# Two-layer decoder trunk on one core: the input handed over in both layouts, and a first stage without transposes

## The reference

```python
def gdn_mixer(x, w_in, conv_w, a_log, dt_bias, norm_g, w_out):
    h = x @ w_in
    qkv, z, b_raw, a_raw = split(h)               # q, k, v, z: 8 heads x 128 columns each; b, a: 8 columns each
    qkv = silu(causal_depthwise_conv(qkv, conv_w))    # 4 taps per channel
    ...
    beta = sigmoid(b_raw)
    g = -exp(a_log) * softplus(a_raw + dt_bias)
    o = gated_delta_rule(q, k, v, beta, g)        # chunked recurrence per head
    return (rms_norm(o, norm_g) * silu(z)) @ w_out
x = layer_norm(ALPHA * x + y)                     # the residual uses x again, with positions along the rows
```

## Time and profile before

| | us |
|---|---|
| median of 3 runs | 1806.77 (1806.12 to 1807.46) |
| the profiled execution's own time | 1807.62 |
| its span, first to last instruction | 1805.9 |
| TensorE busy | 1708.3 (95% of the span) |
| DVE, ACT, POOL busy | 867.9, 790.4, 300.7 |
| mean granted TensorE clock | 0.978 of full speed |

### The profile page before, as it was taken

The page is one execution under the profiler, slowest core; times in us unless marked ns, Lnnn a source line. Parts: engine busy times, 40 slices in busy tenths (PEclk is TensorE's granted clock), DMA queues, the critical chain, the costliest instruction groups (busy, mean ns, idle before and its releaser), DMA issues. The chain is left out here.

```text
span 1805.9 us, 29014 instructions
## 1 busy us (share of the span) xinstructions
PE 1708.3 (95%) x11245; PEld 1303.6 (72%) x11245; DVE 867.9 (48%) x1664; ACT 790.4 (44%) x1296; POOL 300.7 (17%) x243
## 2 busy tenths in 40 slices
PE   6999999999999897979989998999999999898898
PEld 4777777787777775858877887666666665687787
DVE  3667576674766635653330300344444454565433
ACT  3557465574655732142231311465655665430411
POOL 2222132221322251200000000222221221012000
PEclk9999999999999998989989999999999999899899
DMA  5121110211101121141130201111111101050311
GB/s 131 48 53 36 31 48 12 49 37 34 48 13 38 57 95 59 35 125 44 53 107 1 71 25 36 43 33 45 44 33 42 43 22 41 19 164 28 117 44 50
DMA packets 113080, 92.87 MB, mean 51 GB/s; under 512 B 19696, under 2 KB 95664, under 8 KB 112944
## 3 DMA queue, kind: packets, MB, share of 16 engines
q1 hardware_dynamic: 112944, 91.02, 17.8%
HBM read 82.51 MB, written 8.49 MB: 50 GB/s over the span
## 5 line engine op out<-in xcount | busy, mean ns | idle before, releaser
L481 PE MATMUL gdn_unit<-part_hi,gdn_w_hi 128*128 128x512 f32 x512 | 231.8, 453 | 0.2 <-DVE gdn_w_lo L837 0.2
L483 PE MATMUL gdn_unit<-part_hi,gdn_w_lo 128*128 128x512 f32 x512 | 201.5, 394 | 0.0
L482 PE MATMUL gdn_unit<-part_lo,gdn_w_hi 128*128 128x512 f32 x512 | 200.5, 392 | 0.0
L2090 DVE CUSTOM_DVE_ANT_0 fa_probs<-fa_scores,fa_decay 128x896 f32<-128x896 f32 (+7 forms) x128 | 97.0, 758 | 121.2 <-PE fa_scores L1902 73.6
L877 DVE SCALAR_TENSOR_TENSOR x<-gdn_raw,gdn_taps,x 128x512 f32<-128x512 f32 x144 | 132.4, 919 | 21.9 <-ACT x L696 17.2
L1854 PE MATMUL fa_unit<-part_hi,fa_w_hi 128*128 128x512 f32 x256 | 115.0, 449 | 4.8 <-ACT fa_qk L2001 3.4
L446 POOL TENSOR_TENSOR gdn_w_lo<-ring,gdn_w_hi 128x1024 fp32r<-128x1024 f32 x31 | 74.6, 2408 | 265.2 <-ACT gdn_w_hi L676 265.2
L2036 ACT ACTIVATE fa_probs_t<-fa_turned 128x512 f32<-128x512 f32 (+1 forms) x96 | 52.3, 545 | 139.3 <-PE fa_turned L1919 138.7
L483 PEld LDWEIGHTS gdn_unit<-part_hi,gdn_w_lo 128*128 128x128 f32 x512 | 96.1, 188 | 21.5
L2030 ACT ACTIVATE fa_probs<-fa_probs,fa_top 128x896 f32<-128x896 f32 (+7 forms) x128 | 99.4, 777 | 22.6 <-DVE fa_top L2090 18.9
L481 PEld LDWEIGHTS gdn_unit<-part_hi,gdn_w_hi 128*128 128x128 f32 x512 | 96.8, 189 | 16.8 <-issue 3.6
(11 more groups left out here) (307 smaller groups left out, 3622.1 us busy)
## 6 DMA issues: line engine op xcount, KB each, us to landing
ring<-in_gdn_w_in_dram SPq DMA_DIRECT2D x32, 512.0 KB, 4.2
ring<-in_ple_w_gate_dram SPq DMA_DIRECT2D x32, 256.0 KB, 3.0
ring<-in_fox_w_in_dram SPq DMA_DIRECT2D x32, 256.0 KB, 3.3
ring<-in_fox_w_in_dram SPq DMA_DIRECT2D x16, 512.0 KB, 4.7
fa_decay<-c_rows_scratch SPq DMA_DIRECT2D x64, 128.0 KB, 3.0
in_x_tile<-in_x_dram SPq DMA_DIRECT2D x8, 512.0 KB, 6.8
gdn_g_bc<-g_rows_scratch SPq DMA_DIRECT2D x8, 512.0 KB, 8.6
x_scratch<-x SPq DMA_DIRECT2D x8, 512.0 KB, 2.9
```

Source lines behind the costliest of these rows:

```text
L481: pe.matmul(out, w_hi[:, j % 2, k, :], xh[:, k, ts], start=(k == 0), stop=False)
L482: pe.matmul(out, w_hi[:, j % 2, k, :], xl[:, k, ts], start=False, stop=False)
L483: mm = pe.matmul(out, w_lo[:, j % 2, k, :], xh[:, k, ts], start=False, stop=(k == KT - 1))
```

## The change

The kernel gets x twice: as before, and as `x_t`, with channels along the rows. `transpose_input` is gone, and with it its barrier and the loads `to_gdn`. In `delta_net`:

- SP issues, in this order: `load(0)`, x_t's tile 0, the b/a columns, tiles 1 to 7 of x_t, `load(1)`, the two short vectors, the taps, the gain. The raw tiles lie in buffers that are unused at that time (`x_raw`).
- ScalarE makes `high_part(0)`, then the high part of each tile, with `ab_hi` behind tile 0; VectorE makes the low parts in the same order. The wait for the short vectors moves to where they are used.
- GpSimd makes the constants here, and signals `masks_made`.
- TensorE warms up with 18 matmuls in place of 9, and then `first_products` makes, tile by tile, what steps 0 to 15 of iteration 0 made (both halves of q of head 0) and the b/a products: 12 matmuls for each tile.
- Gates are turned at step 18, summed at 36, rows turned at 40; ScalarE copies the product at step 16.

```diff
-def transpose_input(nc, x, c, xh, xl, after):
...
-AT_GATES = 2
-AT_GATES_TURNED = 6
-AT_G_SUMS = 24
-AT_G_ROWS = 28
+AT_GATES = 16
+AT_GATES_TURNED = 18
+AT_G_SUMS = 36
+AT_G_ROWS = 40
...
+        def x_raw(k):
+            return qkvz_space[:, 4 + k] if k < 4 else o_t[:, k + 1] if k < 7 else qkvz_space[:, 3]
...
+            load(0)
+            for k in range(KT):
+                sp.dma_start(x_raw(k), turned_input[0, k * P:(k + 1) * P, :]).then_inc(x_loaded[k], 16)
+                if k == 0:
+                    sp.dma_start(ab_raw, w_in[:, 4 * H * DK:4 * H * DK + 2 * H].rearrange("(k p) n -> p k n", p=P)
+                                 ).then_inc(ab_loaded, 16)
+            load(1)
...
+            constants_program(pool, step, c, ident_made, masks_made)
...
+            def first_products():
+                pe.wait_ge(w_low, 1)
+                for k in range(KT):
+                    pe.wait_ge(x_low, k + 1)
+                    for half in range(2):
+                        out, ts = unit[half][:], slice(half * HALF, (half + 1) * HALF)
+                        pe.matmul(out, w_hi[:, 0, k, :], xh[:, k, ts], start=(k == 0), stop=False)
+                        pe.matmul(out, w_hi[:, 0, k, :], xl[:, k, ts], start=False, stop=False)
+                        mm = pe.matmul(out, w_lo[:, 0, k, :], xh[:, k, ts], start=False, stop=(k == KT - 1))
+                        if k == KT - 1:
+                            mm.then_inc(unit_made, 1)
+                    if k == 0:
+                        pe.wait_ge(gate_low, 1)
+                    for half in range(2):
+                        out, ts = w2[0:2 * H, half * HALF:(half + 1) * HALF], slice(half * HALF, (half + 1) * HALF)
+                        pe.matmul(out, ab_hi[:, k], xh[:, k, ts], start=(k == 0), stop=False)
+                        pe.matmul(out, ab_hi[:, k], xl[:, k, ts], start=False, stop=False)
+                        mm = pe.matmul(out, ab_lo[:, k], xh[:, k, ts], start=False, stop=(k == KT - 1))
+                mm.then_inc(ab_product, 1)
...
             def gate_work(s):
                 if s == AT_GATES_TURNED:
+                    pe.wait_ge(masks_made, 1)
                     pe.wait_ge(ab_copied, 1)
...
-            warm_up(pe, c, w0)
+            pe.wait_ge(ident_made, 2)
+            warm_up(pe, c, w0, 18)
+            first_products()
...
-                    if it < H:
+                    if it < H and 8 * it + s // KT >= 2:
                         project(it, s)
...
             high_part(0)
-            act.wait_ge(gate_loaded, 48)
-            step(act.activation(ab_hi, ab_raw, ACT.Copy), gate_high)
+            for k in range(KT):
+                act.wait_ge(x_loaded[k], 16)
+                step(act.activation(xh[:, k], x_raw(k), ACT.Copy), x_high)
+                if k == 0:
+                    act.wait_ge(ab_loaded, 16)
+                    step(act.activation(ab_hi, ab_raw, ACT.Copy), gate_high)
             act.wait_ge(small, 16 * (TAPS + 1))
...
-            dve.wait_ge(gate_high, 1)
-            step(dve.tensor_tensor(ab_lo, ab_raw, ab_hi.bitcast(F32), ALU.subtract), gate_low)
+            for k in range(KT):
+                dve.wait_ge(x_high, k + 1)
+                step(dve.tensor_tensor(xl[:, k], x_raw(k), xh[:, k].bitcast(F32), ALU.subtract), x_low)
+                if k == 0:
+                    dve.wait_ge(gate_high, 1)
+                    step(dve.tensor_tensor(ab_lo, ab_raw, ab_hi.bitcast(F32), ALU.subtract), gate_low)
...
-                transpose_input(nc, a["x"], c, part_hi, part_lo, to_gdn)
-                delta_net(nc, c, ring, to_gdn, to_ple[0], part_hi, part_lo, gates, gdn_in, a["gdn_dt_bias"][0],
+                delta_net(nc, c, ring, a["x_t"], to_ple[0], part_hi, part_lo, gates, gdn_in, a["gdn_dt_bias"][0],
```

More of the change, by code:

```diff
@@ L80, in __call__, with constants_program @@
         self.engine.wait_ge(sem, self.value[sem])
-def constants_program(pool, step, c, ident_made):
+def constants_program(pool, step, c, ident_made, masks_made):
     def select(ap, compare, fill, base, pattern, multiplier):
@@ L93, in constants_program @@
     step(pool.memset(c["tri"][:], 1.0))
-    select(c["tri"][:], ALU.is_ge, 0.0, 0, [[1, P]], -1)
+    step(pool.affine_select(out=c["tri"][:], in_=c["tri"][:], compare_op=ALU.is_ge, fill=0.0, base=0,
+                            pattern=[[1, P]], channel_multiplier=-1), ident_made)
     step(pool.memset(c["ones"][:], 1.0))
@@ L114, in constants_program @@
             select(ap, ALU.is_ge, 0.0, HALF_P * part + s - 1, [[2 * s, nb], [0, s]], -1)
-        step(pool.tensor_tensor(m, m, upper, ALU.add))
+        step(pool.tensor_tensor(m, m, upper, ALU.add), masks_made if level == LEVELS - 2 else None)
 def warm_up(pe, c, bank, rounds=9):
@@ L254, with delta_net @@
 OUT_ROWS = tuple(range(10, 26, 2))
-def delta_net(nc, c, ring, ahead, after, xh, xl, gates, w_in, gate_bias, a_log_dram, conv_w, norm_g, g_rows_dram, qkvz_space, o_t,
+def delta_net(nc, c, ring, turned_input, after, xh, xl, gates, w_in, gate_bias, a_log_dram, conv_w, norm_g, g_rows_dram, qkvz_space, o_t,
               w_out, residual):
@@ L293, in delta_net @@
         w_loaded = [sem(f"w_loaded{n}") for n in range(2)]
+        x_loaded = [sem(f"x_loaded{k}") for k in range(KT)]
+        ident_made, masks_made, x_high, x_low = sem("ident_made"), sem("masks_made"), sem("x_high"), sem("x_low")
+        ab_loaded = sem("ab_loaded")
         g_loaded = sem("g_loaded")
@@ L668, in high_part @@
             def high_part(j):
-                if j < 2:
-                    ahead.arrive(act)
-                else:
-                    act.wait_ge(w_loaded[j % 2], 16 * (j // 2))
+                act.wait_ge(w_loaded[j % 2], 16 * (j // 2 + 1))
                 if j >= 2:
@@ L2168, in rows @@
             return [(ring[:, n], w[n * P:(n + 1) * P, :]) for n in range(2)]
-        to_gdn = ahead("gdn", columns(gdn_in, (0, H * DK)))
         to_mix = ahead("m1", rows(a["fox_w_out"][0]))
@@ L2207 @@
 _INS = ["x", "p", "ln_g", "ln_b", "ple_w_gate", "ple_w_proj", "gdn_w_in", "gdn_conv_w", "gdn_a_log", "gdn_dt_bias",
-        "gdn_norm_g", "gdn_w_out", "fox_w_in", "fox_b_f", "fox_q_norm_g", "fox_k_norm_g", "fox_w_out"]
+        "gdn_norm_g", "gdn_w_out", "fox_w_in", "fox_b_f", "fox_q_norm_g", "fox_k_norm_g", "fox_w_out", "x_t"]
 def kernel(**inputs):
@@ L2217 @@
     nc = _bacc.Bacc("TRN2", target_bir_lowering=False, num_devices=1)
+    inputs["x_t"] = _np.swapaxes(inputs["x"], 1, 2)
     arrays, args = {}, {}
```

16 lines of the change are left out of this document (5 added, 11 removed).

## The result

The changed kernel takes 1792.05 us, the median of four executions (1790.94 to 1793.57), against 1806.76 for the kernel before: a ratio of 0.9912, with a 95% interval from 0.9901 to 0.9924. It is faster by 14.7 us where 16.7 were forecast, and lies inside the range of 1786 to 1796. The profiled execution took 1791.22 us with a span of 1789.5, which is 16.4 less than before.

What follows compares the result with a forecast made beforehand. TensorE, busy 95% of the span, was taken as the bound. Reaching step 16 at 31.7 instead of 50.06 us gives 18.4; less 0.66, 0.5, 0.2 and 0.3 leaves 16.7: 1790.1 us, range 1786 to 1796.

Steps and rivals of the forecast that it cites:

- Start at 9.4, end at 31.7: TensorE's first product at 9.4 us (8.6 to 10.4); its 96 first matmuls take 22.3 us and end at 31.7.
- Pace of TensorE: In the first products TensorE needs 2.78 us a tile, more than ScalarE, VectorE or the transfers, so it sets the pace.
- rival of bunched loads: x_t's tiles land late and together; TensorE starts at 15 us, total 1795.7, up to 1801 us; chance 0.12.
- Warm-up at no cost: Warm-up ends at 8 to 8.5 us, before the first product; products at full clock, nothing charged.
- low-clock rival: Low clock through first products: full form 22.3 us more, 1812.4, chance 0.02; short form 3.5 us, 1793.6, chance 0.06.
- Small loads and block 1's weights: Block 1's low part ready at 30.7 against 31.7, 0.2 us charged; rival: slower taps, 3 to 7 us stall, chance 0.15.
- The copy of b/a: At step 18 TensorE's transposes wait 0.5 us (0 to 1.0) for ScalarE's copy of the b/a product.
- The upper end of 1793.8 us: Total time if TensorE starts at 10.4 us and all stalls occur.
- (d): Gate chain 12 steps later in iteration 0; the sum of squares comes about 0.3 us later.
- 17.5 us less before the sums of squares: Sign of being right: the sums of squares of head 0 come 17.5 us earlier than in the kernel before.
- later stages equal to within 2 us: Sign of being right: stages behind the changed start take the same time to within 2 us.
- 1.5 us either way: Allowance for later stage boundaries shifting against the clock's falls, from three runs that differ by 1.3 us.

Runs made afterwards that it cites:

- e3: Changed kernel with 9 warm-up rounds in place of 18: median 1795.46 us, ratio 0.9928.
- e5: Changed kernel with iteration 0's sums of squares of k at step 51 in place of 45: median 1788.70 us, ratio 0.9895.
- e6: Changed kernel with gate sums at step 33, gate rows turned at 37, and iteration 0's sums of squares at 51: median 1787.79 us, ratio 0.9889.
- e10: Changed kernel with b/a products as one block behind q, and VectorE's gate chain at step 24 in place of 18: median 1789.15 us, ratio 0.9901.
- e11: The kernel before, no edit, run again for a second profile: 1808.61 us.

## Why the prediction was right, and where it was not

**Start at 9.4, end at 31.7.** Measured 9.50 and 31.59. Tile 0 and weights landed as estimated. The timeline of ACT, DVE and POOL of the changed kernel:

```profile
5.33 1.06 ACT L637 ACTIVATE gdn_w_hi<-ring 128x1024 fp32r<-128x1024 f32 x1 [3.25 <-DMA ring<-in_gdn_w_in_dram]
6.50 1.28 DVE L803 TENSOR_TENSOR gdn_w_lo<-ring,gdn_w_hi 128x1024 fp32r<-128x1024 f32 x1 [4.66 <-ACT gdn_w_hi L637]
6.97 1.06 ACT L733 ACTIVATE part_hi<-x 128x1024 fp32r<-128x1024 f32 x1 [0.58 <-DMA x<-in_x_t_dram]
8.13 1.22 DVE L806 TENSOR_TENSOR part_lo<-x,part_hi 128x1024 fp32r<-128x1024 f32 x1 [0.35 <-ACT part_hi L733]
...
13.87 2.31 POOL L85 TENSOR_SCALAR_AFFINE_SELECT upper_mask<-upper_mask 128x32 f32<-128x32 f32 x2
...
26.36 1.06 ACT L637 ACTIVATE gdn_w_hi<-ring 128x1024 fp32r<-128x1024 f32 x1 [8.96 <-DMA gdn_gain<-in_gdn_norm_g_dram]
27.60 2.40 POOL L394 TENSOR_TENSOR gdn_w_lo<-ring,gdn_w_hi 128x1024 fp32r<-128x1024 f32 x1 [5.58 <-ACT gdn_w_hi L637]
```

VectorE hardly waited for GpSimd (1.28 us for 1.22); it was GpSimd that did, with two selects in 2.31 us that took 0.5 to 0.7 alone. The price fell on the engine with slack, and the masks were ready at 22.0, long before their use. The lock that the Trainium skill describes (SBUF — State Buffer, "SBUF: two separate sides") agrees with these rows, and its sentence that whoever starts first blocks the other agrees with the row of 38.48 us below, where GpSimd had started at 38.30.

**Pace of TensorE.** Right: 96 matmuls in 22.1 us, no gap. The rival of bunched loads falls. ScalarE began a tile each 1.28 us.

**Warm-up at no cost.** The clock was up at 9.50, right; but the warm-up took 7.24 us and ended 0.05 ahead of the first product, where I had it end at 8 to 8.5. In the nine other profiles with 18 rounds it took 5.67 to 6.43 us and ended at 7.9 to 8.7, about as forecast. It is no free margin: e3 shows that without the second half the low-clock rival, in its short form, comes true. There slow products start 0.43 us apart and not 0.46, so the full form would have cost some 19 us and not 22.3.

**Small loads and block 1's weights.** Gain landed near 26.3 where I took 27; the low part was ready at 30.0, 1.6 ahead of its use. That rival falls as well.

**The copy of b/a.** 0.53 us where 0.5 was charged.

**Slips that moved nothing.** The 72% read as the busiest other engine are TensorE's own weight loads; the busiest other engine is VectorE with 48%. The upper end of 1793.8 us is not what its stated ends add up to, which is 1793.1. "17.5 us less before the sums of squares" does not follow from the terms, which leave 16.7. In the row read as "both ended together", VectorE ended 0.28 us behind GpSimd.

**The step that failed is (d),** "the sum of squares ... comes about 0.3 later". The loss between step 16 and the mark was 5.9 us (18.47 to 12.6) where all terms together had 1.7. I had moved the gate chain by 12 steps and looked at the engine that waits, ScalarE, but had not added up VectorE's program behind step 16. In the kernel before the gate chain was done ahead of units 0 and 1; in the new one these rows stand in a row on VectorE:

```profile
38.48 2.28 DVE L142 TENSOR_SCALAR o_t<-o_t 128x64 f32<-128x64 f32 x1
...
43.39 7.50 DVE L848 SCALAR_TENSOR_TENSOR x<-gdn_raw,gdn_taps,x 128x512 f32<-128x512 f32 x7
50.92 0.22 DVE L832 COPY gates_g<-gdn_w 128x64 f32<-128x64 f32 x1
...
52.67 3.90 DVE L848 SCALAR_TENSOR_TENSOR x<-gdn_raw,gdn_taps,x 128x512 f32<-128x512 f32 x5
```

The first is a 0.2 us operation that stood behind GpSimd's low part (2.40 us from 38.30). All edited kernels have it too (2.27 or 2.28 us), so no run shows the chain without it. But it is no added cost. In the kernel before two of GpSimd's low parts fell on convolutions of VectorE, of which three take 2.33 us alone:

```profile
50.60 6.82 DVE L877 SCALAR_TENSOR_TENSOR x<-gdn_raw,gdn_taps,x 128x512 f32<-128x512 f32 x6
...
63.24 4.34 DVE L877 SCALAR_TENSOR_TENSOR x<-gdn_raw,gdn_taps,x 128x512 f32<-128x512 f32 x3 [1.71 <-ACT x L696]
```

That is 4.2 us of standing behind GpSimd before, and 4.1 after (2.1 in the chain, 2.1 in the seven convolutions). What is new is the chain itself: 8.2 us of VectorE's time from 35.15 on, of which only 0.5 lay behind step 16 before. VectorE copies the sums at 50.92, TensorE has waited 1.25; the last convolution that the squares need ends at about 54.2, 22.6 us behind step 16 where it was 17.5 before, and TensorE waits 3.22. Then comes a price that no term had: behind this wait the clock fell, and the sums cost 1.06 us more and the products behind them some. e5 (the wait removed, 3.7 us), e6 (1.3 us for the order) and e10 (the order of VectorE's program, 3.6 us) show each part.

**The end on the right number is partly luck.** The missed 4.2 us were given back by 3.8 us in unchanged later stages of the profiled execution. Two of the prediction's own signs of being right failed with them: 17.5 us less before the sums of squares (14.3), and later stages equal to within 2 us. I had allowed 1.5 us either way there, from three runs; 13 executions of the kernel before spread over 5.1, and the same code took from 1713.5 to 1719.2 us over all profiles. The clock accounts for it: 75.1 us at the lower level behind the mark before and 68.3 after are 3.4 of the 3.8 us. Whether the change itself makes the clock fall less often behind it is not shown: e6 took 1786.6 to 1791.7 us with one code, at mean clocks of 0.979 and 0.977. What decides between a fall and none in the same code stays open.

## What to carry to other kernels

When work is moved to another step of a hand-written schedule, write down the whole program of each in-order engine behind the new place, not only the instruction that waits: the queue of the engine with the least slack sets the loss. A wait of TensorE costs its length and often the clock as well, here behind most waits of 2.1 to 3.7 us; putting independent products ahead of the wait (e5) takes both away with two changed step numbers. Judge such edits by a landmark in the trace ahead of the common code, because the spread of the whole time can be larger than what they bring, and look at the granted clock before you explain a difference between executions of common code.

## What was not expected of the hardware

- The same 36 warm-up matmuls took from 5.67 to 7.24 us in ten profiles, and the granted clock column showed 1.00 in the first 6 us although they were as long as slow ones (a mean of 421 ns from 4 to 6 us of the changed kernel, against 279 in the warm-up of the kernel before).
- The length of a wait alone does not decide whether the clock falls. At the sums it fell behind waits of 3.19, 3.22 (three profiles) and 3.67 us, and in e10 behind one of only 2.11, but not in e3 behind 3.22 and not in the kernel before behind 1.93. At the old barrier it stayed up through 3.70 us and fell in 3.44 us in e11. The Trainium skill (TensorE: Matmul & The Clock Gate, Part 1) says that the number of slow matmuls at the start of one kernel varies from run to run; the ten warm-ups above agree.
- Behind 5.2 MB of queued loads SP took 5.36 us to issue a vector of 4 KB that had taken 0.74 before, but the taps only 9.15 in place of 7.53, and the gain landed within 26.3 us of the start.
